# Strassen-form products for the query, key, value and gate projections of the forgetting attention

## The reference

```
h = _rmsnorm(x, norm_w) * (1 + scale) + shift
proj = jnp.einsum("bsd,de->bse", h, w_in)
z_ssm, xbc, dt_raw, q, k, v, z_att, f_logit, g_logit = jnp.split(proj, offsets, axis=-1)
y_att = _fox_branch(q, k, v, z_att, f_logit, b_f)
    # for each head and each block of 128 queries:
    logits = q k^T * scale + f_cum[query] - f_cum[key], causal
    probs = softmax(logits);  o = probs v;  y = o * silu(z_att)
merged = g_ssm * (y_ssm @ w_proj_ssm) + g_att * (y_att @ w_proj_att)
```

## Time and profile before

| | us |
|---|---|
| three timed runs | 2067.74, 2067.75, 2071.47 (median 2067.75) |
| the profiled execution | 2069.03 |
| its span, first to last instruction | 2067.5 |
| PE busy, whole program | 1954.4 (95%) |
| DVE busy / ACT busy | 995.4 (48%) / 759.2 (37%) |
| PE granted clock, mean | 0.978 of full speed |

### The profile page before, as it was taken

How to read it: one execution, slowest core, us unless ns; L and a number is a source line. 1 busy time by engine, 2 the same in 40 slices (tenths; PEclk the granted TensorE clock), 3 DMA queues, 4 the chain that set the end, 5 groups by cost and what they waited for, 6 DMA issues and landing times. The chain is left out here.

```text
span 2067.5 us, 26015 instructions
## 1 busy us (share of the span) xinstructions
PE 1954.4 (95%) x9712; PEld 1570.7 (76%) x9712; DVE 995.4 (48%) x1217; ACT 759.2 (37%) x1137; POOL 156.5 (8%) x311
## 2 busy tenths in 40 slices
PE   6899999998999999999999999959999998999997
PEld 3678787776787887888788788837777777888786
DVE  4576544545422334333433344469333344555865
ACT  4422333244313434444343433243144345442422
POOL 0000110000100000000000000002100001110100
PEclk8899999999999999999999999989999999999998
DMA  7441655634431111111111343332321111211302
GB/s 280 180 73 42 102 97 109 101 107 128 142 112 51 33 48 30 41 41 41 51 30 41 118 147 112 82 114 81 101 65 35 42 30 26 71 36 30 130 29 92
DMA packets 165319, 166.35 MB, mean 80 GB/s; under 512 B 11402, under 2 KB 143938, under 8 KB 163970
## 3 DMA queue, kind: packets, MB, share of 16 engines
q1 hardware_dynamic: 151746, 116.11, 18.2%
q0 software_dynamic: 13504, 49.29, 10.6%
HBM read 132.22 MB, written 33.16 MB: 80 GB/s over the span
## 5 line engine op out<-in xcount | busy, mean ns | idle before, releaser
L288 PE MATMUL acc<-ha_hi,w_hi 128*128 128x512 f32 x1152 | 468.7, 407 | 4.2 <-ACT stash L301 3.0
L288 PE MATMUL acc<-ha_hi,w_lo 128*128 128x512 f32 x1152 | 451.9, 392 | 0.0
L288 PE MATMUL acc<-ha_lo,w_hi 128*128 128x512 f32 x1152 | 450.3, 391 | 0.0
L288 PEld LDWEIGHTS acc<-ha_hi,w_hi 128*128 128x128 f32 x1152 | 217.5, 189 | 49.0 <-issue 5.1
L288 PEld LDWEIGHTS acc<-ha_hi,w_lo 128*128 128x128 f32 x1152 | 216.8, 188 | 47.7
L288 PEld LDWEIGHTS acc<-ha_lo,w_hi 128*128 128x128 f32 x1152 | 217.6, 189 | 41.8
L257 DVE TENSOR_TENSOR w_lo<-w_raw,w_hi 128x1024 fp32r<-128x1024 f32 x128 | 157.6, 1231 | 140.5 <-ACT w_hi L253 137.3
L271 PE MATMUL acc<-ha_hi,w_hi 128*128 128x512 f32 x592 | 187.5, 398 | 27.6 <-DVE ha_lo L1740 13.5
L271 PE MATMUL acc<-ha_lo,w_hi 128*128 128x512 f32 x592 | 184.8, 394 | 0.0
L271 PE MATMUL acc<-ha_hi,w_lo 128*128 128x512 f32 x592 | 184.2, 392 | 0.0
L271 PEld LDWEIGHTS acc<-ha_hi,w_hi 128*128 128x128 f32 x592 | 110.6, 190 | 58.1 <-issue 15.7
(11 more groups left out here) (437 smaller groups left out, 2755.7 us busy)
## 6 DMA issues: line engine op xcount, KB each, us to landing
w_raw<-in_w_in SPq DMA_DIRECT2D x99, 512.0 KB, 3.9
w_ada<-in_w_ada SPq DMA_DIRECT2D x8, 1024.0 KB, 11.8
acs_bc<-acs_scr POOLq DMA_DIRECT2D x8, 1024.0 KB, 16.3
w_raw<-in_w_out SPq DMA_DIRECT2D x11, 512.0 KB, 3.9
x_tok<-in_x SPq DMA_DIRECT2D x8, 512.0 KB, 6.7
xt_scr<-xt SPq DMA_DIRECT2D x1, 4096.0 KB, 22.6
w_ada_g<-in_w_ada SPq DMA_DIRECT2D x8, 512.0 KB, 9.8
z_scr<-stash SPq DMA_DIRECT2D x8, 512.0 KB, 11.2
```

The source lines that it names most:

```text
L288: mm = pe.matmul(acc[:, 0, half * HALF:(half + 1) * HALF], w[:, n % 2, k, :], x[:, k, half * HALF:(half + 1) * HALF], start=(k == 0 and i ...
```

## The change

The tiles of a head go by pairs, (q, k) and (v, z). A pair of tiles and the two halves of the features and of the tokens make a 2 x 2 block product, which is done with seven half products instead of eight (Strassen's form in Winograd's variant). A half product is 4 slices x 3 passes of 512 columns, 12 matmuls, as a part was: 14 per head for 16. To have them:

- Sums of the activations (`t1`, `t2`, `t3`, each 4 slices x 512 tokens, high and low part) are made once, before head 0, by DVE and ACT; a fourth, `t4`, overwrites a quarter of `ha_hi` and `ha_lo`. They lie where `ya_hi` and `ya_lo` lay, so that the heads' outputs go to memory during the stage and come back at its end (7 rows of 512 KB for the high part and 7 for the low).
- Sums of the weights (four operations of DVE for each pair) are made in `w_raw` and `w_sum`; the splits go by half tiles (128x512), 14 of ACT and 14 of DVE per head for four whole ones each.
- Each product is read as it ends: ACT copies products 0, 3, 7 and 10 to `kept1` or `kept5`, DVE adds the ten others to what was kept (`read`), and four more additions bring in `kept5`. Product q waits until product q - 2, which lay in its bank, has been read.
- Both weight tiles of a pair are loaded together, when the last product of the pair before has been split.

The core of the diff:

```diff
-        def fox_fills(t):
-            return range(3) if t == 0 else range(2 * t + 2, 2 * t + 4) if t < 5 else [t + 7]
+        FIRST = N_FOX + 4
+        PER_PAIR, PER_HEAD = 7, 14
+        ROLES = ["a11", "a12", "s2", "s1", "s3", "s4", "a22"]
+        SLOT = [0, 1, 2, 3, 0, 1, 2, 3, 0, 1, 2, 3, 2, 3]
+        FILLS_AT = [[0, 1, 2], [4], [5, 6], [7, 8], [9], [10], [11], [12]]
+        ACT_READS = [0, 3, 7, 10]
+        DVE_READS = [1, 2, 4, 5, 6, 8, 9, 11, 12, 13]
...
+        def product_hi(act, q, h):
...
+            act.wait_ge(mm_done, FIRST + slot_before(q) + 1 + PER_HEAD * h)
+            act.activation(product_slot(w_hi, q), weight_of(q), ACT.Copy).then_inc(hi_done, 1)
+        def product_lo(dve, q, h):
+            dve.wait_ge(hi_done, FIRST + q + 1 + PER_HEAD * h)
+            dve.tensor_tensor(product_slot(w_lo, q), weight_of(q), product_slot(w_hi, q).bitcast(F32), ALU.subtract
+                              ).then_inc(lo_done, 1)
+        def weight_sums(dve, pair, h):
+            a11, a21, a22 = w_raw[:, W0, K1, :], w_raw[:, W1, K1, :], w_raw[:, W1, K2, :]
+            dve.drain()
+            raw_landed(dve, 0, pair, h)
+            raw_landed(dve, 1, pair, h)
+            dve.tensor_tensor(a21, a11, a21, ALU.subtract)
+            dve.drain()
+            dve.tensor_tensor(w_sum[:, :, :], a22, a21, ALU.subtract)
+            dve.drain().then_inc(w_summed, 1)
+        def weight_sums_in_place(dve):
...
+            dve.tensor_tensor(a11, a11, w_sum[:, :, :], ALU.add)
+            dve.tensor_tensor(a12, a12, w_sum[:, :, :], ALU.subtract)
+            dve.drain().then_inc(w_summed, 1)
...
+            def load_pair(offs, pair, h):
+                products_split(sp, pair, h)
+                for i, off in enumerate(offs):
+                    sp.dma_start(w_raw[:, (W0, W1)[i], :, :], cols(w_in, off)).then_inc(w_loaded[(W0, W1)[i]], 16)
...
+                def fill(q):
+                    pe.wait_ge(lo_done, FIRST + q + 1 + PER_HEAD * h)
+                    pe.wait_ge(*read_count(q - 2, h))
...
+                    for k in range(KH):
+                        for i, (w, x) in enumerate(((w_h, hi), (w_h, lo), (w_l, hi))):
+                            mm = pe.matmul(bank(q), w[:, k, :], x[:, k, :], start=(k == 0 and i == 0),
+                                           stop=(k == KH - 1 and i == 2))
+                    mm.then_inc(mm_done, 1)
...
                 for t in range(NT):
-                    for part in fox_fills(t):
-                        fill(part)
+                    for q in FILLS_AT[t]:
+                        fill(q)
...
@@ act_5, a head @@
                 exps(0)
+                keep(0)
                 for t in range(NT):
                     if t + 1 < NT:
                         exps(t + 1)
+                    if t == 0:
+                        product_hi(act, 3, h)
+                        product_hi(act, 4, h)
...
+                    if t == 4:
+                        product_hi(act, 11, h)
+                    copies(t)
...
+                    if t == 5:
+                        keep(10)
+                        product_hi(act, 12, h)
+                    if t == 6:
+                        product_hi(act, 13, h)
...
+                    for q in range(3):
+                        product_hi(act, PER_HEAD + q, h)
                 act.wait_ge(y_gated, 2 * h + 4)
-                act.activation(row(ya_hi, h), y_head[:, :], ACT.Copy).then_inc(x_hi_done, 1)
+                    for i in range(2):
+                        e = act.activation(y_hi[i][:, :], y_head[:, i * HALF:(i + 1) * HALF], ACT.Copy)
...
@@ dve_5, a head @@
+                    if t == 0:
+                        product_lo(dve, 3, h)
+                        product_lo(dve, 4, h)
+                        read(1)
+                        read(2)
...
+                    if t == 2:
+                        weight_sums(dve, 1, h)
+                        product_lo(dve, 7, h)
+                        product_lo(dve, 8, h)
+                        read(5)
+                        read(6)
...
                     if t == 5:
+                        product_lo(dve, 12, h)
...
                         gate(0)
+                    if t == 6:
+                        read(11)
+                        product_lo(dve, 13, h)
+                        add_kept5(1)
...
+                    weight_sums(dve, 2, h)
+                    product_lo(dve, PER_HEAD, h)
+                    product_lo(dve, PER_HEAD + 1, h)
+                    weight_sums_in_place(dve)
+                    product_lo(dve, PER_HEAD + 2, h)
+                read(13)
                 gate(1)
...
@@ pe_6 @@
-            project(pe, N_MIX2, ya_hi, ya_lo, after=LO_SPLITS[5])
+            pe.wait_ge(y_back, Y_BACK + 4 * 16)
+            project(pe, N_MIX2, ya_hi, ya_lo, last=LO_SPLITS[5] + KT)
```

More of the change, by code:

```diff
@@ L267, in project @@
                     pe.wait_ge(x_lo_done, after + k + 1)
+                if last is not None and k == KT - 1:
+                    pe.wait_ge(x_lo_done, last)
                 passes = [(w_hi, x_hi), (w_hi, x_lo), (w_lo, x_hi)]
@@ L1435, in exps, with copies, keep @@
                                    accum_out=row_sum[:, t % 2:t % 2 + 1]).then_inc(exp_done, 1)
-                def read_next(t):
-                    i, half = divmod(t, 2)
-                    read_half(act, N_FOX + 4 + i, half, FILLS2 + 4 * h + i, next_tiles[i], adv=2 * h)
-                    if half:
-                        act.drain().then_inc(nxt_ready, 1)
+                def copies(t):
+                    for c, a, b in fox_chunks(t):
+                        act.wait_ge(p_turned, FC * h + c + 1)
+                        act.activation(prob_t[:, t % 2, a:b, :], work[:, 2 + c % 2, 0:(b - a) * P], ACT.Copy).then_inc(p_copied, 1)
+                def keep(q):
+                    act.wait_ge(mm_done, FIRST + q + 1 + PER_HEAD * h)
+                    if ROLES[q % PER_PAIR] == "a11":
+                        act.wait_ge(*read_count(q - 5, h))
+                        e = act.activation(kept1[:, :], bank(q), ACT.Copy)
+                    else:
+                        act.wait_ge(*read_count(q - 4, h))
+                        e = act.activation(kept5[:, :], bank(q), ACT.Copy)
+                    e.then_inc(pair_read, 1)
                 act.wait_ge(v_turned, h + 1)
                 act.activation(v_tok[:, :, :], work[:, 2:4, :], ACT.Copy).then_inc(v_ready, 1)
+                act.wait_ge(pair_added, 10 * h + 10)
                 act.activation(silu_za[:, :], next_tiles[3][:, :], ACT.Silu)
@@ L1503, in gate, with halves, read, add_kept5 @@
                     dve.tensor_tensor(y_head[:, s], acc[:, 1, s], silu_za[:, s], ALU.mult).then_inc(y_gated, 1)
+                def halves(q):
+                    tile0, tile1 = next_tiles[2 * (q // PER_PAIR)], next_tiles[2 * (q // PER_PAIR) + 1]
+                    return tile0[:, T1], tile0[:, T2], tile1[:, T1], tile1[:, T2]
+                def read(q):
+                    c11, c12, c21, c22 = halves(q)
+                    out, kept = {"a12": (c11, kept1[:, :]), "s2": (c12, kept1[:, :]), "s3": (c21, c12),
+                                 "s4": (c12, c12), "a22": (c21, c21)}[ROLES[q % PER_PAIR]]
+                    dve.wait_ge(mm_done, FIRST + q + 1 + PER_HEAD * h)
+                    if ROLES[q % PER_PAIR] == "a12":
+                        dve.wait_ge(*read_count(q - 1, h))
+                    dve.tensor_tensor(out, bank(q), kept, ALU.add)
+                    dve.drain().then_inc(pair_added, 1)
+                def add_kept5(pair):
+                    c11, c12, c21, c22 = halves(PER_PAIR * pair)
+                    dve.wait_ge(*read_count(PER_PAIR * pair + 3, h))
+                    dve.tensor_tensor(c12, c12, kept5[:, :], ALU.add)
+                    dve.tensor_tensor(c22, c21, kept5[:, :], ALU.add)
+                    dve.drain()
                 dve.wait_ge(fbc_loaded, 16 * h + 16)
@@ L1518, in head @@
+                read(13)
                 gate(1)
+                dve.drain()
                 dve.wait_ge(x_hi_done, SPLITS[5] + h + 1)
-                dve.tensor_tensor(row(ya_lo, h), y_head[:, :], row(ya_hi, h).bitcast(F32), ALU.subtract
-                                  ).then_inc(x_lo_done, 1)
-            with dve.Fori(0, FOX_HEADS) as h:
+                if last:
+                    dve.wait_ge(late_saved[0], LATE_SAVED)
+                    dve.tensor_tensor(ya_lo[:, FOX_HEADS - 1, :], y_head[:, :], ya_hi[:, FOX_HEADS - 1, :].bitcast(F32), ALU.subtract
+                                      ).then_inc(x_lo_done, 1)
+                else:
+                    for i in range(2):
+                        s = slice(i * HALF, (i + 1) * HALF)
+                        dve.tensor_tensor(y_lo[:, s], y_head[:, s], y_hi[i][:, :].bitcast(F32), ALU.subtract)
+                    dve.drain().then_inc(x_lo_done, 1)
@@ L1524, in dve_5 @@
+            with dve.Fori(0, FOX_HEADS - 1) as h:
                 head(h)
```

(2 more changed lines are left out.)

288 lines of the change are left out of this document (235 added, 53 removed).

## The result

| | before | after |
|---|---|---|
| median of 4 runs, same chip | 2068.68 us | 2124.91 us |
| lowest to highest | 2067.74 to 2071.47 | 2119.59 to 2127.24 |
| the profiled execution, its span | 2069.03, 2067.5 | 2127.24, 2125.7 |
| PE's granted clock, mean | 0.978 | 0.966 |

The account below looks back on a forecast made before the run. PE bounds the kernel before, but would then wait on DVE's and ACT's in-order lists. Head 0's start, savings and waits, seven heads at +6.1, last seam -1.3 and end +5 give +52: 2120 us, range 2088 to 2145.

Parts of the forecast that it names:

- saved matmuls, a head: Filling in the attention loop: 14 products for 16 parts, 24 matmuls of 0.228 fewer, 5.5 us a head saved.
- product 3: Step 0: PE waits 1.0 us for DVE's read of product 1, behind the splits of products 3 and 4.
- product 7: Step 3: PE waits 0.8 us for the read of product 5, behind the second pair's weight sums and both loads.
- values of step 4: PE waits 1.1 us for ACT's copies, behind `exps(5)` and the high part of product 11.
- values of step 6: Steps 5 to 6: PE waits 3.1 us for ACT's copy, behind `exps(7)` and DVE's longer list.
- product 2 behind `kept`: Between two heads: product 2 waits 5.2 us for ACT's `keep(0)`, some 2.9 in head 0.
- start of head 0: Before the loop: activation sums on DVE delay a weight split, so head 0 starts 2.7 us later.
- end: After the last head: outputs' low parts reload from memory before stage 6's projection; +5 us, range 3 to 13.
- The clock in the loop: After the wait between heads, product 2 runs at half clock, up to 2.7 us more; counted as 0.4 a head.
- Smaller waits: Rival: waits in the loop real but smaller, a head of 68 to 69.5 us, total 2090 to 2105; chance 0.15.
- payment in full: Rival: clock cost unabsorbed, 2.3 more a head, or reload at the slow rate, 8 more; 2140 to 2155, chance 0.11.
- The faster case: Rival: PE stays the bound in the loop and only the saved matmuls count; 2033 us, chance 0.07.

Follow-up runs that it names:

- the nine kernels: The changed kernel and the eight reorderings of its DVE and ACT lists that leave the start as it is; 2047.14 to 2137.65 us.
- the best kernel: Changed kernel with all list reorderings, silu late, next head's logits ahead, products 5 and 1 read ahead of splits, early reload; 2047.14 us, 0.9898 of the kernel before.
- the two moves alone: Changed kernel with only `gate(1)` and output high parts ahead of weight work, 2105.65 us; or only product 12's low part and `gate(0)` behind step 7's logits, 2107.82.
- Both together: Changed kernel with `gate(1)` before weight work, product 12's low part and `gate(0)` later, and product 11's high part behind step 4's copies; 2076.20 us, ratio 1.0040.

## Why the prediction was right

It said 2120 in a range of 2088 to 2145, slower, by PE's waits; 2124.9 was measured. Its steps against the trace:

| step | predicted | measured |
|---|---|---|
| saved matmuls, a head | -5.5 | -5.45 (with nothing else changed) |
| product 3 | 1.0 | none, hidden by the half clock; 0.7 once that was gone |
| product 7 | 0.8 | 0.70 |
| values of step 4 | 1.1 | 0.90 |
| values of step 6 | 3.1 | 2.84 |
| product 2 behind `kept` | 5.2 (head 0: 2.9) | 5.0 to 5.3 in four heads; 3.9 and 3.1 where the clock had fallen at step 6 of the head before; 4.2 in the last head, 2.15 in head 0 |
| a head | 72.0 | 71.4 (mean of seven), 69.7 to 73.4 |
| request of a pair of loads to their landing | 5.8 | 5.9, to the first sum |
| DVE busy in a head | 44 | 42.7 |
| start of head 0 | +2.7 | +6.2 |
| heads together | +44.4 | +46.9 |
| end | +5 | +5.1 |

**The mechanism** was right at each place, and four of five waits to 0.3 us (product 2's in four of its eight cases). The half clock was right in kind and partly wrong in place, as told below. The experiments show it by their reverse: with the same arithmetic, and the lists in another order, 76 us came back.

The Trainium skill ("VectorE: DVE Perf Modes", The TRN2 errata) gives a measured 691 and 2291 ns for a float32 addition of two tensors at 512 and 2048 elements, and the trace agrees: 0.69 us for the half tiles, 2.29 for the activation sums. The prediction says that DVE's half tiles from SBUF alone had no row, and works out the long ones. Both had rows in the kernel before, outside the attention: 680 ns (L1040) and 2292 ns (L1672). Its prices were right all the same.

**The mis-sized term is the start**: "DVE begins at 603.3; a split, seven of these and a split end at 621.8 ... So head 0 starts 2.7 later". The split ended at 621.95, as said. But PE had stood for 3.2 us, and the clock cost, which I counted between the heads, was not counted here. PE in order of time at the third projection, then its clock in three windows of one us:

```profile
622.00 1.22 PE L281 MATMUL acc<-ha_hi,w_hi 128*128 128x512 f32 x2 [3.22 <-DVE w_lo L265]
623.02 1.05 PE L281 MATMUL acc<-ha_lo,w_hi 128*128 128x512 f32 x2
...
628.11 0.62 PE L281 MATMUL acc<-ha_lo,w_hi 128*128 128x512 f32 x2
```

```profile
622.00:623.00 1.00, 1.00 (x2) 0.50 0.00 0
625.00:626.00 1.00, 1.00 (x3) 0.50 0.00 0
628.00:629.00 1.00, 1.00 (x5) 0.98 0.00 0
```

From 622.00 to 628.11 seven pairs of matmuls ran in 6.11 us; at full clock they take 7 x 0.455 = 3.2. So 3.2 of waiting and 2.9 of half clock make 6.1 of the 6.2. (Head 0 begins at 644.2 to 648.8 in the nine kernels with this start, but most of that scatter is older than stage 5. Counted from PE's first projection of head 0, it begins 45.2 us later before the change and 50.2 to 51.7 in the nine, so 5.0 to 6.5 for the predicted 2.7: the wait is 3.2 in each, and most of the rest the clock.)

**The end** is right in size, and partly by luck: the reload's wait is smaller than the sum needs, and the clock, which the sum leaves out here, makes up for it. The wait for the reload is 3.66 us where 2.1 had been waited for ACT, +1.6; then the projection runs at half clock, +2.9 of the other 3.5:

```profile
1226.12 1.22 PE L281 MATMUL acc<-ya_hi,w_hi 128*128 128x512 f32 x2 [3.66 <-DMA ya_lo<-y_lo_scr]
1227.14 1.05 PE L281 MATMUL acc<-ya_lo,w_hi 128*128 128x512 f32 x2
...
1232.24 0.63 PE L281 MATMUL acc<-ya_lo,w_hi 128*128 128x512 f32 x2
```

**The clock in the loop** was taken at 0.4 a head. In the head from 861.88, product 2 lasts 878.47 - 874.25 = 4.22 for 2.73, 1.5 more, and the wait of 1.0 for product 3 is gone in exchange: 0.5 net. What I did not foresee is that the wait at step 6 puts the clock down too, in three of the eight heads. Such a head, at its step 6:

```profile
1209.11 3.36 PE L1558 MATMUL acc<-prob_t,v_tok 128*128 128x128 f32 x14 [2.83 <-ACT prob_t L1636]
1212.11 0.77 PE L1533 MATMUL acc<-ha_hi,w_hi 128*128 128x512 f32 x1
```

The values take 1212.11 - 1209.11 = 3.00 where the head above has 1.58, and product 12 takes 1.4 more as well. PE then comes to product 2 of the next head later, and waits less there (3.9 and 3.1 for 5.2), so the chain of DVE and ACT, which doesn't know PE's clock, takes part of it back. This is most of why the heads scatter between 69.7 and 73.4. In the last head, where no product 2 follows, nothing takes it back: these 2.8 us are why it is 8.0 longer where the other seven are 5.6 longer in the mean.

**The rivals.** Smaller waits and payment in full are both refuted in the loop by its mean of 71.4, though the clock's part at start and end leans to the second. The faster case named its own condition, waits of less than 4.5 us a head; the change has 9.9. The last kernels pass that point (2.1 us of idle time a head in the best) and end on the other side, at 2047 where the rival said 2033. In the best kernel's profiled execution, 2054, some 17 of the 21 us above 2033 are the 2.1 that a head takes above the floor, and most of the rest is the start.

## What to carry to other kernels

Before an engine's work is cut at the price of more small operations elsewhere, follow the in-order lists of the others through one period and sum the waits; shares of busy time (DVE 60%, ACT 40%) say nothing on it. When such a wait shows, don't move the last operation before it: find the point that its whole chain hangs on (here the landing of two loads), and move out of the way what doesn't depend on it. And a matmul stream that waits may pay twice: in this stage every wait of 3.1 us or more was followed by the half clock, those between 2.1 and 2.9 us in part of the cases, and the clock cost up to 2.9 us beyond the wait.

## What the runs showed of the hardware that was not expected

- Waits of 2.8 us at step 6 put the granted clock down in three heads of the change and left it in five; in the kernels with the copy of product 0 early and with the gate first, they did so in five and in six of eight. Windows of 10 us behind two such waits, the first with, the second without:

```profile
775.00:785.00 10.00, 7.18 (x30) 0.66 0.47 134
847.00:857.00 10.00, 7.15 (x46) 1.00 0.36 117
```

The work ahead of both is the same. In head 0 a wait of 2.15 us was enough:

```profile
657.78 0.50 PE L1533 MATMUL acc<-t_hi,w_hi 128*128 128x512 f32 x1 [2.15 <-ACT kept L1643]
```

```profile
660.00:661.00 1.00, 1.00 (x3) 0.50 0.00 0
```

In the kernel before, PE waited 2.06 us at the end of stage 5 and the clock stayed at 1.00. The Trainium skill ("TensorE: Matmul & The Clock Gate", What's actually happening) says that the chip's look at activity runs freely and does not start with the kernel, so that the same work can meet it at another phase. That would fit; no run here tests it, and the cause stays open.

- How long the half clock lasts differs too: 2.7 us behind the wait of 5.21 (874.25 to 876.98), but 6.1 behind those of 3.22 and 3.66. In the nine kernels the same wait of 3.2 us at the start costs some 1.5 to 3 us more by it. The clock's cost is not one price.
- The clock couples waits that are far apart: taking out one long wait left most of the half clock in place, and taking out both gave 10 us more than the two moves alone (rows under "Both together").
- Not tried: the version with neither the start's nor the end's cost, which by the terms above (6.2 and 5.1) I estimate at some 10 us below 2047.
